# Six turns of the second block made by trips through memory and 32x32 block transpositions instead of TensorE transposes

## The chip, the cores and the metric

The kernel runs on one core of one Trainium2 chip. The metric is the time of one execution on the device in microseconds (us), median of several. PE is TensorE, DVE VectorE, ACT ScalarE, POOL GpSimd, SP SyncE; P is 128.

## The reference

The program computes a model of two blocks in fp32 on 256 tokens of width 1024. The first block has two layers of four mixers, a dense feed-forward part and a mixture of eight experts. The second block has two layers again, and each computes four branches of width 512 from one projection of the normalised input and joins them with one output projection:

```
y_ret = retention(rope(rq), rope(rk), rv) * silu(rg)
y_ssd = rmsnorm(ssd(silu(conv(xbc))) * silu(z)) * norm_g
y_stick = stick_breaking_attention(sq, sk, sv) * silu(sg)
y_mem = attention(mq, memory keys, memory values) * silu(mg)
h = h + rmsnorm(concat(y_ret, y_ssd, y_stick, y_mem) @ w_out)
```

`xbc` is 1024 wide: 512 state-space inputs x and two groups of B and C. Within ssd, the x part is used with tokens on the partitions; the convolution runs with features on the partitions.

## The kernel before

The five engines run hand-written instruction streams that meet at semaphores. Weights are fp32 and arrive by SP's DMAs in halves of 128x2048 in a ring of five. ACT rounds each half to its upper part (`split` on ACT, L2066) into one of four slots, DVE leaves the remainder in place (`split` on DVE, L2639), and PE adds three products of rounded operands for each weight: `weigh` (L1062) for tiles whose result has tokens on the partitions, `weigh_wide` (L1117, L1124) for results with features on the partitions. A half's upper part has to be there when PE starts on it, the remainder some 3.7 us later.

`SECOND_TILES` gives the order of the weight tiles in a layer of the second block, `SECOND_JOBS` (L324) the order in which results take the eight PSUM banks in turn: X0 X1 Z DT MQ MG SQ SK SV SG RQ RK RV RG, then the four tiles of the output projection, O1 O3 O2 O0. Between tiles PE does small work: maps (`causal`, L1663 and L1664), their application (`head_apply`, `ssd_apply`, L1669 to L1671), sums for the stick-breaking part (`stick_sums`, L1719, L1721), and turns.

A turn (`turn`, L1131) makes features-on-partitions of a 128x512 tile by four 128x128 transposes on PE into one bank; two such calls turn a 256x512 value. In each layer of the second block PE turns seven values, all by L1135: XT (x of the state-space part after the convolution, from features to tokens), the branches YM (memory), YD (state space), YS (stick-breaking) and YR (retention), and the rotated queries QR and keys KR of retention. Each ends in a bank, from which ACT copies it (XT, QR, KR) or takes its upper part (`y_high`, L2484) with DVE taking the remainder (`y_lower`, L3420).

DVE's stream in a layer is written out by hand in order. The part that matters here, between the splits of RK and O2: `stick_softplus`, `ssd_out(3)`, `y_lower` of YM, the normalisation of the state-space branch (L3603, L3604, then `ssd_n`), `rotate` of RQ (L3459 to L3463), `stick_out(0)`, `stick_softplus(2)`, split RV, `rotate` of RK, `stick_out(1)`, `stick_softplus(3)` (its last instruction, L3439, sets `sb_sp`, on which PE's `stick_sums(3)` waits), `y_lower` of YD, split RG, `stick_out(2)`, `stick_less(3)`, split O1, `stick_out(3)`, split O3, the decay of retention's maps LR0 to LR3 (L3634) with `y_lower` of YS between the second and the third.

POOL does almost nothing in the second block. In the dense feed-forward part of the first block it already carries six turns by another way, `store_rows` (L1950) and `fetch_pieces` (L1953): one DMA writes a 256x512 value to memory, then, when it has landed, four DMAs of 32 partitions each fetch it back so that each 32x32 piece lies in the partitions where its transpose belongs, and one DVE transposition of 32x32 blocks (L2972) finishes it:

```
pool.dma_start(dram.rearrange("(b p) d -> p b d", p=P), v).then_inc(moved_out, 16)
for a in range(QUADS):
    pool.dma_start(shaped(pieces, SEQ // GROUP, n)[GROUP * a:GROUP * (a + 1), :, :],
                   dram[:, n * a:n * (a + 1)].rearrange("(g j) c -> j g c", j=GROUP)).then_inc(fetched, 16)
```

POOL waits in its own order, so a trip starts only when the fetches of the one before have been issued.

Of the kernel before, what the change touches and what calls it, by code (L numbers as in the profile page):

```python
# [299 lines left out]
FFN_TURNS = 6  # L300

def expert_jobs(r):
# [113 lines left out]
def kernel_program(nc, t):  # L416
# [33 lines left out]
    with ctx:  # L450
# [275 lines left out]
        y_lows = [yr_low, yd_low, ys_low, ym_low]  # L726

        bank = [ctx.enter_context(nc.psum_tensor(f"bank{k}", [P, WIDE], F32)) for k in range(NBANK)]
        bias_dram = nc.dram_tensor("bias_by_distance", [MAPS, REL], F32, kind="Internal")
        hn_dram = nc.dram_tensor("normalised_rows", [SEQ, D], F32, kind="Internal")  # L730
        hid_dram = nc.dram_tensor("hidden_rows", [len(FF_PAIRS), SEQ, WIDE], F32, kind="Internal")
# [293 lines left out]
        def _(pe):  # L1025
# [627 lines left out]
            for l in range(LAYERS):  # L1653
# [126 lines left out]
                for b in range(TB):  # L1780
                    turn(f"XT{b}", [xbc[:, k, 3 + b * P:3 + (b + 1) * P] for k in range(4)], l)
# [27 lines left out]
                pe.wait_ge(*drained("XT1", l))  # L1809
# [22 lines left out]
                branch_turn("YM", gm, drained("PM3", l))  # L1832
# [9 lines left out]
                branch_turn("YD", zs, (ssd_n, l + 1))  # L1842
# [3 lines left out]
                for b in range(TB):  # L1846
                    pe.wait_ge(ret_q, at(l, 4, b + 1))
                    turn(f"QR{b}", [rq[:, b, k * P:(k + 1) * P] for k in range(4)], l)
                by_rows("RG", ["RG0", "RG1"])
                head_apply("PS3", sbw[:, 1, :], v2, 3, (sb_w, at(l, 4, 4)))  # L1850
                for b in range(TB):
                    pe.wait_ge(ret_q, at(l, 4, 2 + b + 1))
                    turn(f"KR{b}", [rk[:, b, k * P:(k + 1) * P] for k in range(4)], l)
# [7 lines left out]
                pe.wait_ge(*drained("YM1", l))  # L1861
# [6 lines left out]
                pe.wait_ge(*drained("YS1", l))  # L1868
# [22 lines left out]
        def _(pool):  # L1891
# [101 lines left out]
            for l in range(LAYERS):  # L1993
# [10 lines left out]
                pool.dma_start(ssd_row, t["ssd_norm_g_2"][l].partition_broadcast(P)).then_inc(rows_in, 16)  # L2004


        @block.scalar
        def _(act):
# [434 lines left out]
            for l in range(LAYERS):  # L2443
# [19 lines left out]
                def conv_silu(k):  # L2463
                    act.wait_ge(conv_acc, at(l, 8, 2 * k + 2))
                    for j in range(2):
                        c = 2 * k + j
                        ins = act.activation(xbc[:, c, 3:3 + SEQ], cacc2[:, k % 2, j, :], ACT.Silu,
                                             bias=par[:, 48 + c:49 + c])
                    ins.then_inc(conv_y, 1)
# [56 lines left out]
                copy2(xh[:, 0, :], "XT0")  # L2526
                copy2(xh[:, 1, :], "XT1")
# [3 lines left out]
                copy2(gm[:, 0, :], "MG0", func=ACT.Silu)  # L2531
                copy2(gm[:, 1, :], "MG1", func=ACT.Silu)
# [20 lines left out]
                copy2(g2[:, 0, :], "SG0", func=ACT.Silu)  # L2553
                copy2(g2[:, 1, :], "SG1", func=ACT.Silu)
# [4 lines left out]
                for b in range(TB):  # L2559
                    y_high(3, f"YM{b}", b)  # L2560
# [7 lines left out]
                inv_root(small2[:, 180:184], small2[:, 176:180], 256, ssd_sq)  # L2568
                stick_ln(2)
# [22 lines left out]
                for b in range(TB):  # L2592
                    y_high(2, f"YS{b}", b)
# [1128 lines left out]
```

## Time and profile before

| | |
|---|---|
| median of 3 runs | 2039.76 us (2037.66 to 2040.54) |
| the profiled execution | 2037.43 us, its span 2035.6 us |
| PE busy | 2023.8 us, 99% of the span, 17507 matmuls |
| DVE, ACT, POOL busy | 921.5 us (45%), 665.1 us (33%), 78.3 us (4%) |
| second block | from about 1540 us to the end, two layers of some 250 us |
| PE's granted clock | 0.999 of full |

Durations in the profile are of instructions one by one; PE's are pipelined and overlap, so that the time a group of matmuls takes is read from its start to the start of what follows.

### The profile page before, as it was taken

The numbers are of one execution on the slowest core, as the hardware profiler recorded it, in microseconds if no ns is written. First come the engines' busy times: TensorE is split into PE (matmuls) and PEld (weight loads), VectorE is DVE, ScalarE is ACT, GpSimd is POOL, SyncE is SP. The second block draws the span as 40 slices with busy tenths as digits, with TensorE's granted clock in tenths as the row PEclk, the third lists the DMA queues.
The fourth block names the chain that finished last, engine by engine and source line by source line (L and its number), as shares of the span: only waits on it lengthen the run. The fifth ranks groups of instructions, "written<-read, shape, count | busy, mean of one in ns | idle before, by whom it ended". The sixth has DMA issues, their size and how long they took to land.

```text
span 2035.6 us, 38980 instructions
## 1 busy us (share of the span) xinstructions
PE 2023.8 (99%) x17507; PEld 1348.0 (66%) x17507; DVE 921.5 (45%) x1286; ACT 665.1 (33%) x878; POOL 78.3 (4%) x113
## 2 busy tenths in 40 slices
PE   9999999999999999999999999999999999999998
PEld 6888888888888353434444353535357888888887
DVE  6877555577766110102020111110127777777775
ACT  5575544455655100000000000000005555456452
POOL 4100011000000000000000000000000000000000
PEclk9999999999999999999999999999999999999999
DMA  9654587555545999999999999999997544455342
GB/s 324 155 186 155 198 263 251 199 186 166 189 154 227 410 418 417 410 419 407 420 403 420 404 420 404 419 403 420 406 409 256 187 145 151 155 200 186 125 165 83
DMA packets 161934, 575.64 MB, mean 283 GB/s; under 512 B 13913, under 2 KB 26977, under 8 KB 130786
## 3 DMA queue, kind: packets, MB, share of 16 engines
q1 hardware_dynamic: 151040, 546.74, 71.3%
q0 software_dynamic: 7168, 22.01, 3.5%
q10 hardware_dynamic: 3554, 4.33, 0.6%
q8 instruction: 140, 2.29, 0.5%
q14 instruction: 32, 0.26, 0.0%
HBM read 564.76 MB, written 8.27 MB: 282 GB/s over the span
## 4 chain that ended last, share of the span: by engine, by line
PE 98%; DMA 1%; DVE 0%; ACT 0%; SPq 0%; DVEq 0%; issue 0%; ACTq 0%
PE bank L1062 40%; PE bank L1408 28%; PE bank L1440 13%; PE bank L1117 5%; PE bank L1124 3%; PE bank L1135 2%; PE bank L1068 1%; DMA ring<-moe_w_down 1%; PE bank L1161 0%; PE bank L1663 0%; PE bank L1671 0%; PE bank L1670 0%; PE bank L1691 0%; PE bank L1677 0%; PE bank L1669 0%; DMA ring<-w_in 0%
## 5 line engine op out<-in xcount | busy, mean ns | idle before, releaser
L1062 PE MATMUL bank<-halves_r,x_both 128*128 128x512 f32 x2624 | 606.8, 391 | 0.0
L1408 PE MATMUL bank<-ring,xT 128*32 128x512 f32 (+1 forms) x6144 | 580.4, 539 | 0.0
L1062 PEld LDWEIGHTS bank<-halves_r,x_both 128*128 128x128 f32 x2624 | 490.4, 188 | 102.0 <-issue 1.7
L1408 PEld LDWEIGHTS bank<-ring,xT 128*32 128x32 f32 x6144 | 199.1, 110 | 372.6 <-issue 371.2
L2639 DVE TENSOR_TENSOR halves_r<-ring,halves_r 128x2048 fp32r<-128x2048 f32 x170 | 384.2, 2287 | 129.0 <-ACT halves_r L2066 127.4
L2066 ACT ACTIVATE halves_r<-ring 128x2048 fp32r<-128x2048 f32 x172 | 325.5, 1914 | 189.7 <-DMA ring<-w_in 77.7
L3190 DVE TENSOR_TENSOR arena<-arena,bank 128x512 f32<-128x512 f32 (+1 forms) x48 | 29.7, 621 | 724.7 <-PE bank L1408 723.3
L1440 PE MATMUL bank<-ring,arena 128*32 128x256 f32 x5376 | 292.1, 379 | 0.7 <-DMA ring<-moe_w_down 0.6
L1440 PEld LDWEIGHTS bank<-ring,arena 128*32 128x32 f32 x5376 | 175.4, 110 | 117.3 <-issue 3.6
L2253 ACT ACTIVATE arena<-bank 128x512 f32<-128x512 f32 (+1 forms) x58 | 32.1, 553 | 462.1 <-PE bank L1408 429.9
L2331 ACT ACTIVATE arena<-bank 128x512 f32<-128x512 f32 (+1 forms) x14 | 6.1, 488 | 356.1 <-PE bank L1440 356.1
L1117 PE MATMUL bank<-x_both,halves_r 128*128 128x512 f32 x448 | 107.3, 392 | 0.3 <-DVE x_both L3486 0.3
L1117 PEld LDWEIGHTS bank<-x_both,halves_r 128*128 128x128 f32 x448 | 82.4, 188 | 18.4 <-issue 1.6
L1062 PE MATMUL bank<-halves_r,yT_high 128*128 128x512 f32 x256 | 80.7, 393 | 0.0
L1124 PEld LDWEIGHTS bank<-x_both,halves_r 128*128 128x128 f32 x448 | 57.4, 191 | 2.2
L1124 PE MATMUL bank<-x_both,halves_r 128*128 128x256 f32 x448 | 58.1, 283 | 0.0
L1062 PE MATMUL bank<-halves_r,hidT_high 128*128 128x512 f32 x176 | 54.7, 390 | 0.0
L1062 PEld LDWEIGHTS bank<-halves_r,yT_high 128*128 128x128 f32 x256 | 47.9, 188 | 9.8
L2044 ACT ACTIVATE arena<-bank 128x512 f32<-128x512 f32 x54 | 30.8, 597 | 61.5 <-PE bank L1062 50.0
L1981 POOL DMA_INDIRECT arena<-normalised_rows,arena x21 | 20.0, 951 | 795.2 <-DVEq L3211 791.0
L3194 DVE STREAM_TRANSPOSE arena<-arena 128x512 f32<-128x512 f32 (+1 forms) x48 | 45.8, 1004 | 0.0
L2645 DVE TENSOR_REDUCE arena<-bank 128x256 f32<-128x512 f32 x56 | 35.1, 683 | 13.9 <-PE bank L1124 13.8
(423 smaller groups left out, 1577.9 us busy)
## 6 DMA issues: line engine op xcount, KB each, us to landing
ring<-moe_w_gate_up SPq DMA_DIRECT2D x128, 1024.0 KB, 13.1
ring<-moe_w_down SPq DMA_DIRECT2D x112, 1024.0 KB, 12.3
ring<-w_in SPq DMA_DIRECT2D x99, 1024.0 KB, 5.2
ring<-moe_w_gate_up SPq DMA_DIRECT2D x128, 768.0 KB, 9.1
ring<-w_out SPq DMA_DIRECT2D x24, 1024.0 KB, 4.9
ring<-ffn_w_gate_up SPq DMA_DIRECT2D x20, 1024.0 KB, 5.5
ring<-ffn_w_down SPq DMA_DIRECT2D x11, 1024.0 KB, 5.0
ring<-w_in SPq DMA_DIRECT2D x18, 512.0 KB, 6.1
```

What stands on the lines that cost most here:

```text
L1062: return pe.matmul(o[:, a:a + n], x[:, c, b * P:(b + 1) * P], w[:, k, col:col + n], **flags)
L1117: mm = pe.matmul(shaped(o[:, :], 2, SEQ), w[:, k, j * P:(j + 1) * P], x_pair[:, :, c, :], start=c == 0, stop=False)
L1124: mm = pe.matmul(o[:, 0:SEQ], w[:, k, j * P:(j + 1) * P], xT_high[:, c, :], start=False, stop=c == KC - 1)
L1135: mm = pe.transpose(o[:, k * P:(k + 1) * P], v, order)
L1408: mm = pe.matmul(shaped(o[i][GROUP * z:GROUP * (z + 1), 0:u], u // P, P), xg[:, c, GROUP * i:GROUP * (i + 1)], w[:, q, z, :, :], start=c == 0,
L1440: mm = pe.matmul(o[i // 2][GROUP * q:GROUP * (q + 1), Q_D * (i % 2):Q_D * (i % 2 + 1)], hidT_m[half][:, i, b:b + GROUP], w[:, c, Q_D * q:Q ...
L2044: act.activation(dst, src, func, scale=scale).then_inc(*fr(job))
L2066: act.activation(top_view(half), raw_view(half), ACT.Copy).then_inc(top_in, 1)
L2253: act.activation(dst, out_of(job)[:, 0:n], ACT.Silu).then_inc(*fr(job))
L2639: dve.tensor_tensor(raw_view(half, halves_r), raw_view(half), top_view(half).bitcast(F32), ALU.subtract).then_inc(raw_low_in, 1)
L2645: dve.tensor_reduce(dst, out_of(job)[:, :].rearrange("p (t s) -> p s t", s=SEQ), AX.X, ALU.add).then_inc(*fr(job))
L3194: dve.transpose(hidT_m[half][:, i, :].rearrange("p (t c g) -> p t c g", c=4, g=GROUP), gated[half][:, i, :].rearrange("p (t f c) -> p t c ...
```

## The change

Six of the seven turns of each layer (all but YR) leave PE. PE's transposes, their twelve places in the order of banks and the copies out of the banks go. In their place each value makes the trip on POOL's queue in the order XT, YM, YD, QR, KR, YS, with a store of 512 KB and four fetches of 128 KB; DVE transposes it in one instruction (XT in two), and for the branches ACT and DVE then take upper part and remainder from SBUF, one 128x1024 instruction each. To let the fetches take whole runs, the producers write their value with the columns in another order (`by_quarter`), in runs of 32 elements: ACT's activations for the convolution, MG and SG, DVE's `mem_out`, `stick_out`, `rotate` and the last factor of the state-space norm, which is now two instructions that write to `xh`.

```diff
+SECOND_TURNS = ('XT', 'YM', 'YD', 'QR', 'KR', 'YS')
+def turns_up_to(l, name):
+    return FFN_TURNS + l * len(SECOND_TURNS) + SECOND_TURNS.index(name) + 1
...
     # PE
-                for b in range(TB):
-                    turn(f"XT{b}", [xbc[:, k, 3 + b * P:3 + (b + 1) * P] for k in range(4)], l)
...
-                pe.wait_ge(*drained("XT1", l))
+                pe.wait_ge(pieces_turned, turns_up_to(l, "XT"))
...
-                branch_turn("YM", gm, drained("PM3", l))
...
-                branch_turn("YD", zs, (ssd_n, l + 1))
...
-                for b in range(TB):
-                    pe.wait_ge(ret_q, at(l, 4, b + 1))
-                    turn(f"QR{b}", [rq[:, b, k * P:(k + 1) * P] for k in range(4)], l)
...
-                pe.wait_ge(*drained("YD1", l))
+                pe.wait_ge(rest_in, FFN_TURNS + at(l, 3, 2))
                 out_tile(1, first=True)
-                pe.wait_ge(*drained("KR1", l))
-                pe.wait_ge(*drained("QR1", l))
+                pe.wait_ge(pieces_turned, turns_up_to(l, "KR"))
...
-                branch_turn("YS", g2, drained("PS3", l))
...
     # POOL
+                sources = {"XT": (xh, flat(xbc[:, 0:4, :])[:, 0:TB * WIDE], (conv_y, at(l, 4, 2))),
+                           "QR": (rq, rq, (ret_q, at(l, 4, 2))), "KR": (rk, rk, (ret_q, at(l, 4, 4))),
+                           "YM": (gm, gm, drained("PM3", l)), "YD": (xh, zs, (ssd_n, l + 1)), "YS": (g2, g2, drained("PS3", l))}
+                for name in SECOND_TURNS:
+                    source, pieces, ready = sources[name]
+                    dram = turn_dram.ap()[l, SECOND_TURNS.index(name)]
+                    pool.wait_ge(*ready)
...
+                    store_rows(dram, source)
+                    pool.wait_ge(moved_out, 48 + 16 * turns_up_to(l, name))
+                    fetch_pieces(dram, flat(pieces))
...
     # ACT
+                def y_top(n):
+                    k = turned_order[n]
+                    act.wait_ge(pieces_turned, turns_up_to(l, ("YM", "YD", "YS")[n]))
+                    act.activation(yT_high[:, 4 * k:4 * k + 4, :], branch_whole[n], ACT.Copy).then_inc(y_in, 1)
...
-                for b in range(TB):
-                    y_high(1, f"YD{b}", b)
                 split(("RG", l))
+                y_top(1)
...
     # DVE
+                def y_turn(n):
+                    dve.wait_ge(fetched, 16 + 16 * QUADS * turns_up_to(l, ("YM", "YD", "YS")[n]))
+                    dve.transpose(branch_whole[n].rearrange("p k (g j) -> p g k j", j=GROUP),
+                                  pieces_of(flat(branch_pieces[n]))).then_inc(pieces_turned, 1)
+                def y_rest(n):
+                    k = turned_order[n]
+                    dve.wait_ge(y_in, at(l, 5, n + 1))
+                    dve.tensor_tensor(y_lows[k][:, :, :], branch_whole[n],
+                                      yT_high[:, 4 * k:4 * k + 4, :].bitcast(F32), ALU.subtract).then_inc(rest_in, 1)
...
-                link(dve.tensor_tensor(zs[:, :, :], zs[:, :, :], under(ssd_row, TB), ALU.mult))
+                for b in range(TB):
+                    ins = dve.tensor_tensor(by_quarter(xh[:, b, :]), in_order(zs[:, b, :]), in_order(ssd_row), ALU.mult)
+                link(ins)
...
                 rotate("RQ1", rq, 1)
+                y_rest(0)
...
-                for b in range(TB):
-                    y_lower(1, f"YD{b}", b, 2 + b)
+                y_turn(1)
                 split(("RG", l))
+                y_rest(1)
                 stick_out(2)
                 stick_less(3)
+                head_rows_turn("QR", q2T, rq)
                 split(("O1", l))
                 stick_out(3)
+                head_rows_turn("KR", k2T, rk)
                 split(("O3", l))
                 for hd in range(4):
                     if hd == 2:
-                        for b in range(TB):
-                            y_lower(2, f"YS{b}", b, 4 + b)
+                        y_turn(2)
+                        y_rest(2)
                         split(("O2", l))
```

On PE, between the tiles RK and RV of a layer (names are tiles; `arena` holds most values), before:

```order
L1719 MATMUL bank<-soft_r,ge_r 128x384
L1721 MATMUL bank<-soft_r,sums_r 128x256 x2
L1135 MATMUL bank<-consts,arena 128x128 [waits bank_free5,ssd_n]
L1135 MATMUL bank<-consts,arena 128x128 x3
L1135 MATMUL bank<-consts,arena 128x128 [waits bank_free6,ssd_n]
L1135 MATMUL bank<-consts,arena 128x128 x3
L1062 MATMUL bank<-halves_r,x_both 128x512 [waits top_in,bank_free0,bank_free7]
```

and in the change:

```order
L1730 MATMUL bank<-soft_r,ge_r 128x384
L1732 MATMUL bank<-soft_r,sums_r 128x256 x2
L1062 MATMUL bank<-halves_r,x_both 128x512 [waits top_in,bank_free2,bank_free1]
```

The eight transposes of YD and their wait on `ssd_n` are gone, and the next tile takes other banks.

On DVE, from the end of `stick_softplus(3)` through the splits of RG and O1, before:

```order
L3439 TENSOR_TENSOR soft_r<-arena,soft_r 128x384 [waits dve_step]
L3420 TENSOR_TENSOR yd_low<-bank,yT_high 128x4x128 [waits y_in] x2
L2639 TENSOR_TENSOR halves_r<-ring,halves_r 128x2048 [waits top_in] x2
L3453 TENSOR_TENSOR arena<-bank,arena 128x2x128 [waits bank_full1,bank_free5]
L3445 TENSOR_TENSOR arena<-arena,bank 128x384 [waits bank_full2]
L2639 TENSOR_TENSOR halves_r<-ring,halves_r 128x2048 [waits dve_step,top_in]
```

and in the change:

```order
L3467 TENSOR_TENSOR soft_r<-arena,soft_r 128x384 [waits dve_step]
L3436 STREAM_TRANSPOSE arena<-arena 128x8x4x32 [waits fetched]
L2656 TENSOR_TENSOR halves_r<-ring,halves_r 128x2048 [waits top_in] x2
L3442 TENSOR_TENSOR yd_low<-arena,yT_high 128x1024 [waits y_in]
L3481 TENSOR_TENSOR arena<-bank,arena 128x8x32 [waits bank_full3,bank_free3]
L3473 TENSOR_TENSOR arena<-arena,bank 128x384 [waits bank_full4]
L3498 STREAM_TRANSPOSE arena<-arena 128x8x4x32 [waits dve_step,fetched]
L2656 TENSOR_TENSOR halves_r<-ring,halves_r 128x2048 [waits top_in] x2
```

The transposition of YD stands where its subtractions from the bank stood; the subtraction now comes after the split of RG, and the transposition of QR is new.

On POOL, the last three trips of a layer in the change, where nothing stood before:

```order
L1950 DMA turned_rows<-arena 128x2x512 [waits ret_q]
L1955 DMA arena<-turned_rows 32x8x128 [waits moved_out]
L1955 DMA arena<-turned_rows 32x8x128 x3
L1950 DMA turned_rows<-arena 128x2x512 [waits ret_q]
L1955 DMA arena<-turned_rows 32x8x128 [waits moved_out]
L1955 DMA arena<-turned_rows 32x8x128 x3
L1950 DMA turned_rows<-arena 128x2x512 [waits bank_free7]
L1955 DMA arena<-turned_rows 32x8x128 [waits moved_out]
L1955 DMA arena<-turned_rows 32x8x128 x3
```

They are QR, KR and YS; each first fetch waits for its own store, and each store stands behind the fetches of the trip before.

## Rows read from the trace of the kernel before

**Rows 1.** Busy time, share and instructions of each engine, the page's first part.

```profile
PE 2023.8 (99%) x17507; PEld 1348.0 (66%) x17507; DVE 921.5 (45%) x1286; ACT 665.1 (33%) x878; POOL 78.3 (4%) x113
```

**Rows 2.** The chain that ended last, by engine.

```profile
PE 98%; DMA 1%; DVE 0%; ACT 0%; SPq 0%; DVEq 0%; issue 0%; ACTq 0%
```

**Rows 3.** Waits of PE in the second block: waited for, us, times, longest.

```profile
PE bank L1135 <- DVE xs L2624: 0.6, 1, 0.6
PE bank L1117 <- DVE x_both L3486: 0.3, 1, 0.3
```

**Rows 4.** Timeline of PE, layer 0: start, us, engine, line, tiles; XT, then YM.

```profile
1600.91 1.07 PE L1135 MATMUL bank<-consts,arena 128*128 128x128 f32 x8
1601.82 0.60 PE L1663 MATMUL bank<-arena 128*128 128x256 f32 x2
...
1676.15 1.04 PE L1135 MATMUL bank<-consts,arena 128*128 128x128 f32 x8
1676.95 11.18 PE L1062 MATMUL bank<-halves_r,x_both 128*128 128x512 f32 x48
```

**Rows 5.** The same in layer 1: XT.

```profile
1850.74 1.07 PE L1135 MATMUL bank<-consts,arena 128*128 128x128 f32 x8
1851.65 0.60 PE L1663 MATMUL bank<-arena 128*128 128x256 f32 x2
```

**Rows 6.** Timeline of DVE in layer 0.

```profile
1616.23 0.69 DVE L3356 TENSOR_REDUCE arena<-bank 128x2 f32<-128x512 f32 x1 [4.83 <-PE bank L1677]
...
1676.34 4.49 DVE L2639 TENSOR_TENSOR halves_r<-ring,halves_r 128x2048 fp32r<-128x2048 f32 x2 [0.24 <-ACT halves_r L2066]
...
1683.64 1.28 DVE L3420 TENSOR_TENSOR ym_low<-bank,yT_high 128x512 fp32r<-128x512 f32 x2
...
1687.85 1.23 DVE L3604 TENSOR_TENSOR arena<-arena 128x1024 f32<-128x1024 f32 x1
...
1692.52 0.41 DVE L3460 TENSOR_TENSOR xs<-bank,arena 128x256 f32<-128x256 f32 x1
...
1693.41 0.69 DVE L3463 TENSOR_TENSOR arena<-xs 128x512 f32<-128x512 f32 x1
...
1711.88 0.56 DVE L3439 TENSOR_TENSOR soft_r<-arena,soft_r 128x384 fp32r<-128x384 f32 x1
...
1728.48 0.42 DVE L3453 TENSOR_TENSOR arena<-bank,arena 128x256 f32<-128x256 f32 x1 [4.38 <-PE bank L1671]
...
1740.87 1.21 DVE L3634 TENSOR_TENSOR arena<-bank,arena 128x384 f32<-128x384 f32 x2 [6.20 <-PE bank L1664]
```

**Rows 7.** One DVE transposition of the feed-forward part, min/median/max ns.

```profile
L2972 DVE STREAM_TRANSPOSE arena<-arena x6: 706/1236/1239, 280.2 to 371.8; 128x1024 f32<-128x1024 f32 x5, 128x512 f32<-128x512 f32 x1
```

**Rows 8.** Timeline of ACT: a copy of 128x1024.

```profile
1540.56 1.06 ACT L2489 ACTIVATE arena<-xT 128x1024 f32<-128x1024 f32 x1
```

**Rows 9.** Timeline of PE in layer 0: the last stick-breaking sums, the map LR2.

```profile
1715.09 0.59 PE L1719 MATMUL bank<-soft_r,ge_r 128*128 128x384 f32 x2
...
1753.13 0.59 PE L1663 MATMUL bank<-arena 128*128 128x256 f32 x2
```

**Rows 10.** Timeline of POOL: two of the six trips of the feed-forward part.

```profile
260.82 0.73 POOL L1951 DMA_DIRECT2D hidden_rows<-arena  x1 [42.17 <-DVE arena L2990]
265.79 2.37 POOL L1956 DMA_DIRECT2D arena<-hidden_rows  x4 [4.23 <-DMA hidden_rows<-arena]
280.84 0.72 POOL L1951 DMA_DIRECT2D hidden_rows<-arena  x1 [12.69 <-DVE arena L2990]
288.02 2.33 POOL L1956 DMA_DIRECT2D arena<-hidden_rows  x4 [6.45 <-DMA hidden_rows<-arena]
```

**Rows 11.** Everything on the tile `hidden_rows`: issues in ns, and landings.

```profile
L1956 POOL DMA_DIRECT2D arena<-hidden_rows x24: 582/582/646, 265.8 to 363.3; - x24
...
DMA to landing us min/median/max: 3.0/4.4/6.9
```

**Rows 12.** Busy time by stretch: the feed-forward trips, and layer 0 here.

```profile
250.00:370.00 120.00, 120.00 (x531) 99.41 (x530) 70.75 (x45) 54.90 (x40) 18.36 (x30) 1.00 0.80 256
1560.00:1780.00 220.00, 220.00 (x1192) 189.20 (x1191) 169.76 (x267) 114.11 (x158) 0.53 (x1) 1.00 0.51 165
```

More of the change, by code:

```diff
@@ L726, in kernel_program @@
         y_lows = [yr_low, yd_low, ys_low, ym_low]
+        turned_order = (3, 1, 2)
+        branch_pieces = [gm, zs, g2]
+        branch_whole = [shaped(flat(v), 4, SEQ) for v in (xs[:, 1:2, :], xh, v2)]
         bank = [ctx.enter_context(nc.psum_tensor(f"bank{k}", [P, WIDE], F32)) for k in range(NBANK)]
@@ L730, in kernel_program @@
         hn_dram = nc.dram_tensor("normalised_rows", [SEQ, D], F32, kind="Internal")
+        turn_dram = nc.dram_tensor("turned_rows", [LAYERS, len(SECOND_TURNS), SEQ, WIDE], F32, kind="Internal")
         hid_dram = nc.dram_tensor("hidden_rows", [len(FF_PAIRS), SEQ, WIDE], F32, kind="Internal")
@@ L2466, in conv_silu @@
                         c = 2 * k + j
-                        ins = act.activation(xbc[:, c, 3:3 + SEQ], cacc2[:, k % 2, j, :], ACT.Silu,
-                                             bias=par[:, 48 + c:49 + c])
+                        if c < 4:
+                            dst = flat(xh).rearrange("p (a c b q) -> p c b a q", a=QUADS, c=4, b=TB)[:, c]
+                            src = shaped(cacc2[:, k % 2, j, :], TB, QUADS, GROUP)
+                        else:
+                            dst, src = xbc[:, c, 3:3 + SEQ], cacc2[:, k % 2, j, :]
+                        ins = act.activation(dst, src, ACT.Silu, bias=par[:, 48 + c:49 + c])
                     ins.then_inc(conv_y, 1)
@@ L2552, in _ @@
                 seg_exponential(3)
-                copy2(g2[:, 0, :], "SG0", func=ACT.Silu)
-                copy2(g2[:, 1, :], "SG1", func=ACT.Silu)
+                copy2(by_quarter(g2[:, 0, :]), "SG0", func=ACT.Silu)
+                copy2(by_quarter(g2[:, 1, :]), "SG1", func=ACT.Silu)
                 split(("RK", l))
@@ L2580, in _ @@
                 stick_exp(3)
-                for b in range(TB):
-                    copy2(q2T[:, :, b * P:(b + 1) * P], f"QR{b}")
                 for b in range(TB):
@@ L2589, in _ @@
                 log_exp()
-                for b in range(TB):
-                    copy2(k2T[:, :, b * P:(b + 1) * P], f"KR{b}")
-                for b in range(TB):
-                    y_high(2, f"YS{b}", b)
+                y_top(2)
                 split(("O2", l))
@@ L3462, in rotate, with head_rows_turn @@
                     dve.sem_inc(*fr(job))
-                    link(dve.tensor_tensor(shaped(dst[:, b, :], 4, P), ra, rb, ALU.add))
+                    link(dve.tensor_tensor(by_quarter(dst[:, b, :]), in_order(rope_t[:, 0, :]), in_order(rope_t[:, 1, :]),
+                                           ALU.add))
                     dve.sem_inc(ret_q, 1)
+                def head_rows_turn(name, dst, src):
+                    dve.wait_ge(fetched, 16 + 16 * QUADS * turns_up_to(l, name))
+                    dve.transpose(dst.rearrange("p k (g j) -> p g k j", j=GROUP),
+                                  pieces_of(flat(src))).then_inc(pieces_turned, 1)
                 if l == 1:
@@ L3550, in _ @@
                 split(("SQ", l))
+                dve.wait_ge(fetched, 16 + 16 * QUADS * turns_up_to(l, "XT"))
+                x_pieces2 = flat(xbc[:, 0:4, :])[:, 0:TB * WIDE].rearrange("p (g c b q) -> p b c g q", g=QUADS, c=4, b=TB)
+                for b in range(TB):
+                    ins = dve.transpose(xh[:, b, :].rearrange("p (c g j) -> p c g j", c=4, g=QUADS), x_pieces2[:, b])
+                ins.then_inc(pieces_turned, 1)
                 dve.wait_ge(*full("AC", l))
@@ L3596, in _ @@
                 ssd_out(3)
-                for b in range(TB):
-                    y_lower(3, f"YM{b}", b, b)
+                y_turn(0)
                 dve.wait_ge(ssd_sq, l + 1)
@@ L3603, in _ @@
                     link(dve.tensor_tensor(z, z, over(s2[:, 180 + 2 * b:182 + 2 * b], 256), ALU.mult))
-                link(dve.tensor_tensor(zs[:, :, :], zs[:, :, :], under(ssd_row, TB), ALU.mult))
+                for b in range(TB):
+                    ins = dve.tensor_tensor(by_quarter(xh[:, b, :]), in_order(zs[:, b, :]), in_order(ssd_row), ALU.mult)
+                link(ins)
                 dve.sem_inc(ssd_n, 1)
```

37 lines of the change are left out of this document (20 added, 17 removed), and 6 rows, old and new, of the table SECOND_JOBS.

## The prediction

> **What bounds the kernel.** I read the page first: PE is busy for 2023.8 of 2035.6 us, DVE for 45% and ACT for a third [rows 1]. The chain that ended last says the same more strictly, since it follows releases: 98% of it is PE [rows 2]. So an instruction that leaves PE is worth its time unless PE then has to wait. The view of waits, cut to the second block, tells how near PE is to waiting: it waits twice in some 500 us, for 0.6 and 0.3 us, both ahead of the first turn that the change touches [rows 3]. Last I read the timelines of PE and DVE through one layer. The stretch view shows DVE at 169.8 of 220 us there, 77%, and the DMA engines at 0.51 [rows 12]: DVE, 45% over the whole span, is the engine to watch in this block.
>
> **What is removed from PE.** Each turn is eight transposes. Their own durations overlap, so I take start to start. XT starts at 1600.91 and the next work at 1601.82, 0.91 us; YM at 1676.15 and the next tile at 1676.95, 0.80 us [rows 4]. YD, QR, KR and YS have the same shape and take 0.79 each. A layer thus loses 0.91 + 0.80 + 4 x 0.79 = 4.87 us, and layer 1 shows the same 0.91 for XT [rows 5]. Two layers: 9.74 us, 96 matmuls. The small gaps when PE changes from one kind of work to another stay, because the small work around the turns stays.
>
> **What is added to DVE.** The nearest row for a transposition is the very same operation on the very same shape in the feed-forward part, 1.24 us for 128x1024 [rows 7]. Per layer:
> - YM, YD, YS: the transposition (1.24) takes the place of the two subtractions (1.28, rows 6), and one subtraction of 128x1024 comes later. Its nearest row is L3604, 1.23 us for the same size [rows 6]. Net +1.2 each.
> - QR, KR: +1.24 each. XT: two of 128x512, about 1.4.
> - The norm's last factor, 1.23 us in one instruction, becomes two of 128x512 at 0.69 (L3463), +0.15 [rows 6].
> Together some 7.7 us per layer on an engine with about 50 us idle in it. ACT gets lighter: three pairs of copies from banks go, and each branch has one copy of 1.06 us [rows 8] instead of two. Writing in runs of 32 I take at nothing: L3460 writes 256 elements in four runs of 64 in 0.41 us, at the rate of the contiguous 128x512 in 0.69 [rows 6]. The bounds are 0 and a doubling of every such instruction; the row is much nearer to 0.
>
> **Where DVE's additions lie.** XT's 1.4 us falls before 1616.23, where DVE had been idle for 4.83 us waiting for PE [rows 6]; it costs nothing. The tight place is from 1676 to 1712. It starts with the split of RK at 1676.34, which follows ACT, which follows PE's end of the tile SG; PE is by then earlier by XT's 0.91, and DVE with it. From there DVE has hardly a gap to the end of `stick_softplus(3)`, 1711.88 + 0.56 = 1712.44. The change adds 0.15 and 1.23 less about 0.2 that fills a gap between dependent instructions: 1712.44 - 0.91 + 1.18 = 1712.7, with a release around 1712.8. PE wants this for the sums that began at 1715.09 [rows 9], less XT, YM and YD, 2.50: at 1712.6. So a slack of 2.65 us is spent, and I expect 0.2 us of waiting, in both layers: 0.4 us. What follows on PE, the tile RG, needs its upper half from ACT, whose stream gets there by the same chain but does RG's split before YD's copy now; I add nothing. Behind it DVE has 4.38 us idle before 1728.48 [rows 6], which covers the later subtraction (1.2) and QR's transposition (1.2).
>
> **The trips.** From the store's issue to the first fetch's issue 4.97 and 7.18 us [rows 10]; the last of four fetches is issued 1.75 us later (2.33 less one issue of 0.58, rows 10, 11); it lands 3.0 to 6.9 us after that, 4.4 in the middle [rows 11]. A trip t is so 9.7 to 15.8 us, 12.2 in the middle. The DMA engines were at 0.80 there and are at 0.51 here [rows 12]; the change adds 12 x 0.5 MB per layer, about 27 GB/s on 165, so I lean to the lower half. Weight loads share the DMA engines, but ACT splits most halves several us before PE wants them; I take nothing for it.
> - YD may start when the norm ends, 1689.1, and DVE wants it at 1712.4: 23 us.
> - QR and KR queue behind it on POOL. A trip holds POOL for t - 3.8, so KR lands at about 1689.2 + 3t - 7.6, 1718 at t = 12.2; DVE wants it after 1728.9 - 3.3 = 1725.6.
> - YS is the tightest. It starts when `stick_out(3)` ends (1728.90 before), and DVE wants it after LR1, 1740.87 + 1.21 = 1742.08, of which KR's 0.79 goes: 12.4 us. A later landing makes DVE wait, with the split of O2 and the maps LR2 and LR3 behind it. After landing DVE needs 1.24, ACT's 1.06, 1.23 and O2's 4.49, 8.0 us. LR2 is on PE at 1753.13 + 0.8 before, 1752.4 without KR and YS, which is 23.5 after `stick_out(3)`. So t up to 15.5 costs PE nothing.
>
> **Sum.** 9.74 - 0.4 = 9.3 us. The profiled execution, 2037.43 with a span of 2035.6, becomes 2028.1; it lies 2.3 under the median of 2039.76. On the median: **2030.5**. Its own range, with 0 to 2 us of waiting per layer and the scatter of the runs (2037.66 to 2040.54), is 2028.5 to 2033. What a measurement can tell from no change is about 0.2%, 4.1 us.
>
> **Rivals.**
> 1. DVE becomes the bound in the tight place. If runs of 32 double the instructions that write them, the two of the norm, four of `rotate` and two of `stick_out` add 2 x 0.69 + 4 x 0.69 + 2 x 0.42 = 5.0 us per layer; no slack is left, so all of it reaches PE, 10.0 us in two layers: 2040.5. Half of it: 2035.5. For it: the slack is spent already. Against it: L3460's rate. Chance 0.11, 0.05 of it beyond 2035.7.
> 2. YS lands late, t of 16 to 17. PE waits 1 to 3 us per layer: 2034.5. For it: 15.8 is the feed-forward part's worst. Against it: less traffic here. 0.07.
> 3. Slower. The trips run one behind the other, so lateness adds up: YD, QR, KR, YS in a row land YS at 1689.2 + 4t - 11.4, and PE can do without it until about 1742.4. Beyond t = 16.2 each us of t costs 4 us per layer. The gain of 4.65 per layer is gone at t = 17.4; t = 19 gives 2030.5 + 2 x 11.2 = 2053. For it: nothing of this traffic has been on POOL in this block, beside a DVE at 77%. Against it: 24 issues in the feed-forward part lie at 582 to 646 ns [rows 11], with DVE at 71 of 120 us [rows 12], so neither issue nor landing shows a busy DVE. 0.04.
> The Trainium skill, page "SBUF — State Buffer", section "SBUF: two separate sides", has a rule that speaks for this rival: while DVE runs one of its two-port modes, GpSimd can't write the descriptors of its own DMAs, and they wait. By that rule the trips would be longer than in rows of an idle DVE; the steady 582 ns next to a DVE at 59% does not bear it out.
> 4. The change does less than it says, because PE's transposes ran in time that PE would have waited anyway. With no wait in rows 3 behind them this would show as no change, 2039.8. 0.01.
>
> **How the numbers follow.** Forecast 0.77, rival 1 0.11, rival 2 0.07, rival 3 0.04, rival 4 0.01. Faster by over 0.2%: 0.77, 0.06 of rival 1 and 0.05 of rival 2, together 0.88; slower by over 0.2%: 0.04; within 0.2%: the remaining 0.08. The range from 2028 to 2035.5 holds the forecast, rival 2 and the mild half of rival 1.
>
> **What would show it.** PE has 17411 matmuls and is still at 98 to 99%. No L1135 between the tiles but for YR and the turns of maps. PE waits under 1 us at `stick_sums(3)` and nowhere else. Stores and fetches of `turned_rows` within 16 us per trip. DVE gains some 15 us of busy time, with transpositions of 1.24 us. I am wrong if PE waits several us for `pieces_turned` or `rest_in` (rivals 2, 3), if DVE's instructions in runs of 32 are longer than their twins (rival 1), or if weight halves reach ACT late.

## The result, and the profile after

| | before | changed |
|---|---|---|
| median of 6 runs each | 2037.68 us (2036.49 to 2040.54) | 2027.57 us (2026.15 to 2029.02) |
| ratio, 95% interval | | 0.995 (0.994 to 0.996) |
| profiled execution: time, span | 2037.43, 2035.6 us | 2029.02, 2027.2 us |
| second block, from PE's first work on the step sizes (4 matmuls of 128x8) in its first layer to the end | 2035.6 - 1600.55 = 435.05 us | 2027.2 - 1601.88 = 425.32 us |
| from layer to layer on PE (the same 4 matmuls in the second layer, less those in the first) | 1850.38 - 1600.55 = 249.83 us | 1846.88 - 1601.88 = 245.00 us |

The change makes the kernel 10.1 us faster by the medians, 9.7 us by the trace of the second block. I forecast 9.3. The median lies all the same 0.43 us below the range of 2028.0 to 2035.5, for a reason that has little to do with the change (below). The two last lines of the table are the better measure: what lies ahead of this point wanders by more than a microsecond from run to run (it was reached at 1600.55 before and, in runs of the changed kernel, at 1599.34 to 1601.88), and none of the work that leaves PE is there. Of the kernel before there is one trace, so 435.05 and 249.83 stand on one execution.

The page of the changed kernel, its first part and the chain by engine, which answer to [rows 1, 2]:

```profile
PE 2015.9 (99%) x17411; PEld 1337.9 (66%) x17411; DVE 934.5 (46%) x1296; ACT 658.1 (32%) x860; POOL 114.2 (6%) x173
...
PE 97%; DMA 2%; DVE 1%; ACT 0%; issue 0%; DVEq 0%; POOL 0%; SPq 0%; ACTq 0%; POOLq 0%
```

PE has 96 instructions fewer and is still the chain. DVE has 13 us more (I had said some 15) and POOL 36; what of it reaches PE is looked at below. The waits of PE in the second block are the two of [rows 3], no more:

```profile
PE bank L1146 <- DVE xs L2641: 0.6, 1, 0.6
PE bank L1128 <- DVE x_both L3521: 0.3, 1, 0.3
```

The stretch of [rows 12] in layer 0. The DMA share goes from 0.51 to 0.62 and the traffic from 165 to 202 GB/s, 37 more where I had said some 27; where the other 10 come from was not looked into:

```profile
1560.00:1780.00 220.00, 220.00 (x1184) 188.87 (x1183) 179.93 (x279) 115.40 (x155) 18.55 (x31) 1.00 0.62 202
```

PE around `stick_sums(3)` (L1730, L1732 now), in the timeline: the product before it begins at 1713.74, the sums 0.38 us later, where 0.14 is usual between the same two kinds of work (1701.56 to 1701.70). So PE starts 0.24 us late there, which the view of waits doesn't show, and it is the one new wait. (The ends of matmuls are modelled in the profile, so I go by starts.)

```profile
1701.56 0.38 PE L1675 MATMUL bank<-arena 128*128 128x128 f32 x2
1701.70 0.60 PE L1730 MATMUL bank<-soft_r,ge_r 128*128 128x384 f32 x2
...
1713.74 0.39 PE L1682 MATMUL bank<-arena 128*128 128x128 f32 x2
1714.12 0.62 PE L1730 MATMUL bank<-soft_r,ge_r 128*128 128x384 f32 x2
```

DVE in layer 0. L3467 is the end of the fourth softplus, which PE waits for, L3436 and L3442 the transposition and the subtraction of a branch, L3498 the transposition of QR, L3492 and L3481 the last addition of `rotate` and the product of `stick_out`, which write in runs of 32 now and take the 0.69 and 0.42 us that they took before [rows 6]:

```profile
1706.85 0.69 DVE L3492 TENSOR_TENSOR arena<-xs 128x512 f32<-128x512 f32 x1
...
1709.89 0.42 DVE L3481 TENSOR_TENSOR arena<-bank,arena 128x256 f32<-128x256 f32 x1
...
1713.51 0.56 DVE L3467 TENSOR_TENSOR soft_r<-arena,soft_r 128x384 fp32r<-128x384 f32 x1
1713.98 1.24 DVE L3436 STREAM_TRANSPOSE arena<-arena 128x1024 f32<-128x1024 f32 x1
...
1721.77 1.25 DVE L3498 STREAM_TRANSPOSE arena<-arena 128x1024 f32<-128x1024 f32 x1 [0.24 <-DMA arena<-turned_rows]
...
1739.63 1.25 DVE L3436 STREAM_TRANSPOSE arena<-arena 128x1024 f32<-128x1024 f32 x1 [0.15 <-DMA arena<-turned_rows]
1742.01 1.23 DVE L3442 TENSOR_TENSOR ys_low<-arena,yT_high 128x1024 fp32r<-128x1024 f32 x1 [1.13 <-ACT yT_high L2506]
1743.81 4.49 DVE L2656 TENSOR_TENSOR halves_r<-ring,halves_r 128x2048 fp32r<-128x2048 f32 x2 [0.58 <-ACT halves_r L2083]
1750.51 1.21 DVE L3678 TENSOR_TENSOR arena<-bank,arena 128x384 f32<-128x384 f32 x2 [2.21 <-PE bank L1675]
```

The transposition at 1739.63 is YS. DVE waits for its landing, but only 0.15 us, and 2.21 us of idle time are left before LR2. POOL's store of YS, and the fetch issues of all second-block trips but XT's, in ns (min/median/max):

```profile
1728.02 0.72 POOL L1950 DMA_DIRECT2D turned_rows<-arena  x1 [10.46 <-DVE arena L3481]
```

```profile
L1955 POOL DMA_DIRECT2D arena<-turned_rows x40: 582/582/613, 1666.2 to 1979.2; - x40
```

Stored at 1728.02, transposed at 1739.63: this trip takes 11.6 us at most, where I took 12.2 for the middle. The fetch issues take 582 ns in the median, as in [rows 11], with DVE busy for 82% of the stretch, so this DVE work doesn't make them longer. The rule that I had weighed for rival 3 (the Trainium skill, page "SBUF — State Buffer", section "SBUF: two separate sides") is one on DVE's two-port modes. No row tells how much of DVE's work here ran in one, so the runs neither bear out nor refute the rule itself.

### The profile page after: what moved, and what is told of

The parts are those of the page before. It is cut to its first block, busy times and chain, and to the rows that moved or that the text cites. A ratio compares the mean times of both kernels' runs of the same rounds, so it can differ in the third digit from the quotient of the medians.

```text
span 2027.2 us, 38820 instructions
## 1 busy us (share of the span) xinstructions
PE 2015.9 (99%) x17411; PEld 1337.9 (66%) x17411; DVE 934.5 (46%) x1296; ACT 658.1 (32%) x860; POOL 114.2 (6%) x173
## 4 chain that ended last, share of the span: by engine, by line
PE 97%; DMA 2%; DVE 1%; ACT 0%; issue 0%; DVEq 0%; POOL 0%; SPq 0%; ACTq 0%; POOLq 0%
PE bank L1073 40%; PE bank L1419 29%; PE bank L1451 13%; PE bank L1128 5%; PE bank L1135 2%; PE bank L1146 1%; PE bank L1079 1%; DMA ring<-moe_w_down 1%; DMA ring<-w_in 1%; PE bank L1674 0%; PE bank L1172 0%; PE bank L1681 0%; PE bank L1682 0%; PE bank L1702 0%; PE bank L1688 0%; PE bank L1680 0%
## 5 line engine op out<-in xcount | busy, mean ns | idle before, releaser
L2061 ACT ACTIVATE arena<-bank 128x512 f32<-128x512 f32 x42 | 24.2, 594 | 57.0 <-PE bank L1073 46.3
```

The costliest lines, as they stand in the source:

```text
L2061: act.activation(dst, src, func, scale=scale).then_inc(*fr(job))
```

## The experiments

Eleven runs were made, two of them of the changed kernel itself, in three groups (e1 to e4, e5 to e8, e9 to e11), each group on one chip with the kernel before beside it. The medians of before were 2036.74 us (15 runs) for the first group, 2037.27 (15) for the second and 2037.52 (9) for the third. For each I give the median and, from its trace, the two distances of the table above: from layer to layer on PE, and from the first of these points to the end ("second block"). For the kernel before they are 249.83 and 435.05.

| kernel | median | under before | layer to layer | second block |
|---|---|---|---|---|
| e1_again | 2026.67 | 10.1 | 245.05 | 425.46 |
| e2_rest_later | 2027.37 | 9.4 | 244.64 | 424.65 |
| e3_dve_extra | 2033.33 | 3.4 | 247.94 | 430.79 |
| e4_store_twice | 2044.50 | -7.8 | 256.82 | 445.02 |
| e5_no_trips | 2029.09 | 8.2 | 245.05 | 425.44 |
| e6_ys_twice | 2038.58 | -1.3 | 250.30 | 435.51 |
| e7_ys_on_pe | 2029.65 | 7.6 | 245.92 | 427.26 |
| e8_mem_trips | 2024.90 | 12.4 | 242.94 | 421.18 |
| e9_ys_twice_o2_first | 2026.93 | 10.6 | 245.07 | 425.50 |
| e10_best | 2023.88 | 13.6 | 242.97 | 421.24 |
| e11_again | 2028.24 | 9.3 | 245.03 | 425.35 |

The last two columns repeat within 0.15 us for kernels that do the same work on PE (e1, e5, e9, e11; 0.2 us with the first trace of the changed kernel), while the medians of these four spread over 2.4 us. Small effects are read from the trace.

### The changed kernel again

> The changed kernel, unchanged. My theory: the change gives 9.3 us, as forecast, and the 10.1 us by which the first measured median lay below that of before came partly from the three runs of before that the forecast was set on (2037.66 to 2040.54). So against before, in runs taken side by side, 8.8 to 10.2 us, ratio 0.995 to 0.996. Rival: the sum is mis-sized and the gain is 11 us or more, which would show as a ratio of 0.9946 or less, and as more than 9.8 us in the trace between the start of the second block on PE and the end.

Measured: 10.1 us under before, ratio 0.9953 (0.994 to 0.9967). The same kernel in the third group, e11_again, gave 9.3 us, 0.9957 (0.9943 to 0.997).

> The changed kernel once more, on the same chip and beside the same runs of before as e10_best, so that the two can be set side by side: 9.3 to 10.1 us under before, and 3.5 to 4.5 us over e10_best; from the start of the second block to the end 425.3 to 425.5 us in the trace.

Both lie in or at the edge of what was expected, and no trace of it shows more than 9.8 us. The gain is 9.3 to 10.1 us, and the rival of a gain of 11 us falls. But my theory that the first 10.1 came partly from the runs of before isn't borne out: 15 other runs of before gave 10.1 again.

### Is the tight stretch without slack?

```
                 rotate("RQ1", rq, 1)
-                y_rest(0)
                 stick_out(0)
...
                 split(("RG", l))
+                y_rest(0)
                 y_rest(1)
```

> YM's subtraction (1.22 us) is taken out of DVE's tight stretch and done just ahead of YD's, where DVE is idle. Theory (the stretch from RK's split to the fourth softplus has no slack left, PE waits 0.24 us for it): the gap on PE ahead of stick_sums(3), 0.38 us from start to start now, falls to its usual 0.14; 0.2 to 0.3 us less per layer, 0.5 us in all, 2027.1 where the unchanged kernel shows 2027.6. Rival (the 0.24 us come from something else, such as the matmul queue or the weight load): the gap stays at 0.38, no change in time. Only the trace can tell the two apart, since 0.5 us is less than the scatter of the runs.

PE's timeline of this kernel: the sums follow after 0.14 us. The layer is 0.41 us shorter than in e1_again.

```profile
1712.72 0.39 PE L1682 MATMUL bank<-arena 128*128 128x128 f32 x2
1712.86 0.59 PE L1730 MATMUL bank<-soft_r,ge_r 128*128 128x384 f32 x2
```

The wait is therefore DVE's, and it costs 0.4 us per layer rather than 0.24, more than I had expected: the products right behind the sums move closer too. The medians (2027.37 against 2026.67) don't show it. The opposite edit adds work to the same stretch:

```
+                    for again in range(3 if job in ("RQ0", "RQ1") else 1):
                         link(dve.tensor_tensor(by_quarter(dst[:, b, :]), ..., ALU.add))
```

> Four more instructions of 0.69 us on DVE per layer (the last addition of the rotation of RQ0 and RQ1 is done three times instead of once), 2.8 to 3.0 us per layer in the tight stretch. Theory (no slack is left between DVE's stretch and the fourth stick_sums on PE): PE waits 2.7 to 3.2 us longer per layer ahead of stick_sums(3), or partly at the stick_sums before it; 5 to 6.5 us slower than the unchanged kernel, 2033 to 2034. Rival (there is slack, or gaps between DVE's dependent instructions swallow the addition): 0 to 2 us slower.

Four instructions of 0.69 us more per layer, 2.8 in all, make the first layer 2.89 us longer and the two together 5.3 (430.79 against 425.46); by the medians the kernel is 6.7 us slower than e1_again. Nearly every added microsecond reaches PE. But the place is another than I had written. PE waits in the second block:

```profile
PE bank L1680 <- ACT arena L2501: 3.9, 4, 1.3
PE bank L1730 <- DVE soft_r L3467: 0.5, 2, 0.2
```

PE now waits mainly for the exponentials (L2501) ahead of PS1 and PS2, which ACT can compute only after `stick_less` on DVE. So the stretch feeds PE at several points. How much room each had stands in the timelines of e1_again, the exponential on ACT and the product (L1680) that wants it:

```profile
1695.94 0.51 ACT L2501 ACTIVATE arena<-arena 128x384 f32<-128x384 f32 x1
1697.95 0.38 PE L1680 MATMUL bank<-arena 128*128 128x128 f32 x2
...
1709.88 0.51 ACT L2501 ACTIVATE arena<-arena 128x384 f32<-128x384 f32 x1
1710.78 0.38 PE L1680 MATMUL bank<-arena 128*128 128x128 f32 x2
```

1.5 us ahead of PS1 and 0.4 ahead of PS2, and none at the sums behind PS2. A delay of 2.8 us uses up the first two as well: PE waits 1.29 and 0.81 us there in layer 0.

### Do the trips cost anything?

```
-                for name in SECOND_TURNS:
+                for name in ("XT",):
...
-                    dve.wait_ge(fetched, 16 + 16 * QUADS * turns_up_to(l, name))
+                    dve.wait_ge(*readies[name])
```

> Left out: the stores and fetches of YM, YD, QR, KR and YS; DVE transposes what lies in the buffers as soon as the rows are ready, so that the branches and the retention compute on rows that are not turned. PE, DVE and ACT do the same instructions as in the changed kernel. Theory (with trips of 9 to 12 us the trips cost PE nothing, and their traffic disturbs nobody): within 0.5 us of the changed kernel, and the distance from layer to layer on PE stays at 245.0 us, since the 0.38 us that remain at stick_sums(3) come from DVE's own work. Rival (the traffic of 40 to 50 GB/s delays weight tiles, or landings delay DVE somewhere on the path): 1 to 3 us faster.

This kernel leaves out the stores and fetches of all values but XT, so DVE transposes rows as they lie and the results are not those of the model; the instructions on PE, ACT and DVE are the same. Without ten of the twelve trips the layer takes 245.05 us, as with them, and the second block 425.44 against 425.46. These trips and their traffic are free. (The median, 2029.09, is higher than e1_again's. With traces this equal I read nothing from it.)

### How far are they from costing something?

```
...
                     store_rows(dram, source)
-                    pool.wait_ge(moved_out, 48 + 16 * turns_up_to(l, name))
+                    pool.wait_ge(moved_out, 32 * turns_up_to(l, name) - 64)
+                    store_rows(dram, source)
+                    pool.wait_ge(moved_out, 32 * turns_up_to(l, name) - 48)
```

> Every one of the six turns of each layer stores its rows twice, the second store after the first has landed, so that each trip is longer by some 2.5 to 4 us and GpSimd's queue with it. The values stay the same. Theory (trips are serial; now about 9 to 12 us each, and the last one, YS, has about 4 us to spare before PE waits for its product; XT has more): trips of 12 to 15 us, four of them in a row from YD on, land YS at 1741 to 1750 on the time scale of the changed kernel's trace, and PE waits 0 to 4 us per layer ahead of the first causal product of the retention or ahead of tile O2: 0 to 8 us slower in all, 2 likeliest. Rival of free trips (they never reach PE): within 0.3 us of the unchanged kernel and no new wait of PE in the trace. Rival of tight trips (PE waits at LR0 for KR): more than 8 us slower.

This is far off: 7.8 us slower than before and 17.8 slower than the changed kernel, with its five runs from 2039.7 to 2048.1. My likeliest case was 2, and the rival of more than 8 had PE wait at LR0 for KR, which it doesn't. POOL, DVE and PE in layer 0, and the waits:

```profile
1729.07 0.72 POOL L1950 DMA_DIRECT2D turned_rows<-arena  x1
1737.10 0.72 POOL L1950 DMA_DIRECT2D turned_rows<-arena  x1 [7.31 <-DMA turned_rows<-arena]
1743.67 2.34 POOL L1955 DMA_DIRECT2D arena<-turned_rows  x4 [5.86 <-DMA turned_rows<-arena]
```

```profile
1748.86 1.25 DVE L3440 STREAM_TRANSPOSE arena<-arena 128x1024 f32<-128x1024 f32 x1 [10.02 <-DMA arena<-turned_rows]
...
1757.44 1.01 DVE L3682 TENSOR_TENSOR arena<-bank,arena 128x384 f32<-128x384 f32 x2
```

```profile
PE bank L1680 <- DVE arena L3682: 14.0, 2, 8.9
```

```profile
1758.14 0.77 PE L1680 MATMUL bank<-arena 128*128 128x128 f32 x2 [8.93 <-DVE arena L3682]
...
1763.40 0.55 PE L1073 MATMUL bank<-halves_r,yT_high 128*128 128x512 f32 x1
```

PE waits 8.93 us in layer 0 and 5.1 in layer 1 for LR2's product, which stands on DVE behind YS and the split of O2. KR was late as well (DVE idle for 7.27 us before it), without reaching PE. The second block is 19.6 us longer than in e1_again. 14.0 of these are waits; where are the other 5.5? The stretches, with the granted clock third from the end:

```profile
1749.00:1758.00 9.00, 0.21 (x2) 0.01 (x1) 7.30 (x6) 7.86 (x5) 0.00 (x0) 0.75 0.24 92
1758.00:1763.40 5.40, 5.26 (x19) 4.71 (x20) 3.41 (x19) 0.81 (x3) 0.00 (x0) 0.50 0.00 0
1763.40:1770.00 6.60, 6.60 (x30) 5.46 (x29) 6.57 (x11) 0.00 (x0) 0.00 (x0) 0.97 0.07 24
```

Behind the wait the clock is at 0.50, its lower level of 1.2 GHz, for 5.4 us of work in layer 0: half of it, 2.7 us, is lost on top of the wait, and about as much in layer 1, which makes up the 5.5. To separate YS from the row of trips before it:

```
...
                     store_rows(dram, source)
...
+                    if name == "YS":
+                        store_rows(dram, source)
+                        pool.wait_ge(moved_out, 64 + 16 * l + 16 * turns_up_to(l, name))
```

> Only YS, the last trip of a layer, stores its rows twice, one store after the other; the values stay the same. The trip gets 4 to 5.5 us longer (11.6 us now). From the changed kernel's trace: DVE takes YS within 0.2 us of its landing, and what is behind it has 2.2 us of idle time before LR2 and 1.1 us more until PE wants the product of LR2, 3.3 us together. Theory: PE waits 0.7 to 2.2 us per layer ahead of the third PR, nowhere else, and its clock stays up since the wait is short: 1.5 to 4.5 us slower than the changed kernel, 3 likeliest. Rival (the clock falls with this wait too, as it did behind the waits of 5.1 and 8.9 us, where 2.8 us per layer were lost on top): 6 to 10 us slower. Rival (it was the row of late trips before YS, not YS itself, that cost the time when all stores were doubled): within 0.5 us.

The doubled store of YS alone, one of six in each layer, costs 10.05 us in the second block: the whole gain. POOL's store, DVE's transposition of YS, PE's waits, and the stretches behind the wait in layer 0:

```profile
1725.88 0.72 POOL L1950 DMA_DIRECT2D turned_rows<-arena  x1 [10.39 <-DVE arena L3484]
```

```profile
1744.46 1.25 DVE L3439 STREAM_TRANSPOSE arena<-arena 128x1024 f32<-128x1024 f32 x1 [7.11 <-DMA arena<-turned_rows]
```

```profile
PE bank L1680 <- DVE arena L3681: 6.4, 2, 3.4
```

```profile
1753.70:1755.00 1.30, 1.25 (x11) 1.28 (x12) 1.26 (x5) 0.30 (x1) 0.00 (x0) 1.00 0.00 0
1755.00:1758.60 3.60, 3.60 (x12) 2.83 (x12) 2.84 (x17) 0.42 (x2) 0.00 (x0) 0.53 0.00 0
```

The trip takes 18.6 us, 7.0 more than the 11.6, where I expected 4 to 5.5 more. The second store took 6.9 us to its release, the first 4.5. A busy DVE is not the reason: it was busy for all of the 4.5 us, but for only 1.75 of the 6.9. What is, no run tells. Against 3.3 us of slack that gives a wait of 3.7; measured are 3.41 and 3.02. The rival on the clock holds: it falls after waits of this size too, though only 1.3 us after PE has resumed at 1753.75, and takes 10.05 - 6.43 = 3.6 us from the two layers. The rival that only the row before YS was to blame falls.

### Order instead of speed

```
                     if hd == 2:
+                        split(("O2", l))
                         y_turn(2)
                         y_rest(2)
-                        split(("O2", l))
```

and the same on ACT with `y_top(2)`, both on top of e6_ys_twice.

> YS stores its rows twice as in e6_ys_twice (which cost 10 us in the trace), but ACT and DVE split the tile O2 before they take YS, not after. Theory: the cost of a late YS came from the order of the two engines, not from the lateness: O2's split (3.7 us on ACT, 4.5 on DVE) then fills the time in which DVE waited 7 us for the landing, and only the transposition, ACT's copy and the subtraction, 3.6 us, stand between the landing and LR2's multiplication. With YS on DVE at about 1744.5 and PE wanting LR2's product at 1750.2 PE waits for nothing: the distance from layer to layer returns to 245.0 to 245.3 us, within 1 us of the changed kernel. Rival (O2's tile is not in the ring that early, or ACT is late with it, so that YS now waits behind O2): PE waits again, 2 us or more per layer.

DVE's timeline:

```profile
1739.39 4.48 DVE L2659 TENSOR_TENSOR halves_r<-ring,halves_r 128x2048 fp32r<-128x2048 f32 x2
1746.50 1.25 DVE L3439 STREAM_TRANSPOSE arena<-arena 128x1024 f32<-128x1024 f32 x1 [2.62 <-DMA arena<-turned_rows]
...
1750.51 1.21 DVE L3681 TENSOR_TENSOR arena<-bank,arena 128x384 f32<-128x384 f32 x2 [0.41 <-PE bank L1675]
```

The same slow trip of 18.5 us (1728.01 to 1746.50) costs nothing: 245.07 us per layer, and the kernel is 10.6 us under before, where e6_ys_twice was 1.3 over it. What cost the time was not the late landing by itself but the split of O2 queued behind it. The changed kernel has YS 3.3 us from costing something; in this order 7 us more are harmless.

### What a turn on PE is worth

> YS is turned by PE again, as before the change (8 transposes, two copies by ACT, two subtractions by DVE from the banks); the other five stay with the trips. Theory of the sum (each turn is worth its own time on PE, 0.79 us): the distance from layer to layer on PE rises from 245.0 to 245.8 us, the kernel is 1.6 us slower than the changed one. Rival (YS's trip costs PE something in the changed kernel, so that its removal gave less than 0.79): 0 to 1 us slower.

YS is back on PE, with its old copies and subtractions. The layer is 0.87 us longer, not 0.79, and the second block 1.8 us (427.26 against 425.46) where I expected 1.6. PE's timeline of this kernel, and then of the changed one at the same place:

```profile
1737.28 0.38 PE L1675 MATMUL bank<-arena 128*128 128x128 f32 x2
1737.50 1.04 PE L1146 MATMUL bank<-consts,arena 128*128 128x128 f32 x8
1738.30 0.48 PE L1073 MATMUL bank<-halves_r,yT_high 128*128 128x512 f32 x1
```

```profile
1738.50 0.38 PE L1675 MATMUL bank<-arena 128*128 128x128 f32 x2
1738.64 0.48 PE L1073 MATMUL bank<-halves_r,yT_high 128*128 128x512 f32 x1
```

With the turn 1.02 us pass from the last causal product to the tile, without it 0.14: 0.88. The turn's own start to start is 0.80; the other 0.08 us lie ahead of it, since the transposes begin 0.22 us after the product and the tile only 0.14.

That holds where a turn stood between such a product or sum and a tile. XT stood elsewhere, between the work on the step sizes and the first map. PE there before, around the turn [rows 4], and in the changed kernel:

```profile
1600.55 0.51 PE L1575 MATMUL bank<-arena 128*128 128x8 f32 x4
...
1602.26 0.38 PE L1664 MATMUL bank<-arena 128*128 128x128 f32 x2
```

```profile
1601.88 0.51 PE L1586 MATMUL bank<-arena 128*128 128x8 f32 x4
...
1602.76 0.38 PE L1675 MATMUL bank<-arena 128*128 128x128 f32 x2
```

1.71 us before, 0.88 after: XT's turn was worth 0.83, not the 0.91 from its start to the map's, because the map's own first part, 0.44 us to the next start before [rows 4], now takes 0.52.

### A better version

The memory attention's maps still had 16 transposes per layer on PE. e8_mem_trips turns them by two more trips, each with one DVE transposition of 128x1024, and has YM's subtraction later:

```
-SECOND_TURNS = ('XT', 'YM', 'YD', 'QR', 'KR', 'YS')
+SECOND_TURNS = ('XT', 'AMa', 'AMb', 'YM', 'YD', 'QR', 'KR', 'YS')
...
                 segment_maps(1)
+                head_rows_turn("AMa", pmT, probs[0])
...
                 split(("SG", l))
+                head_rows_turn("AMb", pmT, probs[1])
                 segment_maps(2)
```

> A candidate for a better kernel: YM's subtraction moved as in e2_rest_later, and the four maps of the memory attention (16 transposes on PE per layer, 0.87 us for each pair by the changed kernel's timeline) are turned by two further trips, one per pair, with one DVE transposition of 128x1024 each; ACT loses four copies. DVE has idle time of 4 us and more where the two transpositions go, and the trips have 17 and 20 us. Theory: 1.74 + 0.4 = 2.1 us less per layer on PE, the distance from layer to layer falls from 245.0 to 242.9 us, the kernel is 4.2 us faster than the changed one, 2022 to 2023. Rival (the writes in runs of 32 by ACT, or DVE's added work, push a split back, and PE waits): 0 to 2 us faster, with a wait of PE ahead of the third or fourth PM.

242.94 us per layer, as expected, and 421.18 us for the block, 4.3 less than e1_again. The median is 2024.9 us, 2 over the 2022 to 2023 expected, 12.4 under before, ratio 0.9936 (0.9923 to 0.995). PE's waits are still the same two. DVE finds the first of the two trips landed and takes it without a wait; behind it 0.88 us of idle time are left:

```profile
1639.41 1.24 DVE L3493 STREAM_TRANSPOSE xs<-xs 128x1024 f32<-128x1024 f32 x1
1641.52 2.48 DVE L2657 TENSOR_REDUCE arena<-bank 128x256 f32<-128x512 f32 x4 [0.88 <-PE bank L1136]
```

> e8_mem_trips with O2 split ahead of YS as well. Theory: on fast trips the order of YS and O2 changes nothing for PE, the distance from layer to layer stays at 242.9 us, and the time is that of e8_mem_trips: 4.2 us under the changed kernel in the trace of the second block, 3.5 to 4.5 in the medians. Rival (YS is now taken later and pushes something back): up to 2 us slower than e8_mem_trips.

With O2 ahead of YS as well: 2023.88 us, 4.4 us under the changed kernel beside it (e11_again), 13.6 under before, ratio 0.9932 (0.9919 to 0.9946). In the trace it equals e8_mem_trips (421.24 and 421.18), and the lower median lies within the scatter of the runs. That O2's earlier split makes it less sensitive to a slow trip is shown for the changed kernel (e9_ys_twice_o2_first), not for this one.

## Why the prediction was right, and where it failed

- **What bounds the kernel, and that a turn is worth its time on PE**: right. PE's instructions fell by 96 and the chain is still PE. Rival 4 is out.
- **The six turns, 4.87 us per layer**: too small by 0.3. Without the wait (e2_rest_later) a layer is 249.83 - 244.64 = 5.19 us shorter. I took the time from the first transpose to the next work, 0.79, and wrote that the small gaps around stay; e7_ys_on_pe shows 0.08 us ahead of a turn that goes with it. Laid side by side, the timelines of before and of e2_rest_later give 0.88 us for each of YD, QR, KR and YS, but 0.83 for YM and for XT, where I had 0.80 and 0.91.
- **0.2 us of waiting at `stick_sums(3)` in both layers**: right place, right cause (e2_rest_later), 0.24 us at the wait itself and 0.4 in its effect. e3_dve_extra shows how close the reckoning of "no slack" was, but also that it isn't one point: the exponentials ahead of PS1 and PS2 had only 1.5 and 0.4 us.
- **Sum**: 2 x (5.19 - 0.38) is 9.6 us, the trace 9.7, the forecast 9.3. That it comes so near is partly luck: the turns were 0.6 too small and the wait 0.3 to 0.4 too small, and half of the one cancels against the other.
- **Runs of 32 at nothing** (rival 1): right, 0.69 and 0.42 us as before.
- **The trips** (t of 12.2, YS free up to 15.5): right. YS took 11.6 us in the changed kernel. Delayed on purpose, it gave waits of 3.41 and 3.02 us at t = 18.6 and 18.2, where t - 15.5 is 3.1 and 2.7. For the row of trips rival 3 said that each microsecond beyond 16.2 costs 4; in e4_store_twice YD is stored at 1686.70 and YS transposed at 1748.86, which by its 4t - 11.4 is t = 18.4, so 8.8 us of waiting against 8.93 measured. In layer 1 the same kernel waited 5.1 us. The mechanisms of rivals 2 and 3 exist as described, in kernels made to show them. Their prices were too low: neither had the clock, which took 1.8 to 2.8 us per layer on top.
- **From the sum to the median: here it failed.** "It lies 2.3 under the median of 2039.76. On the median: **2030.5**." That median was of three runs. With three more it was 2037.68, and in 39 further runs of before in three groups 2036.74 to 2037.52; the anchor was 2 to 3 us too high. Of the 2.9 us between 2030.5 and the measured 2027.57 the anchor makes 2.1 and the gain (10.1 by the medians, not 9.3) 0.8. The profiled execution of 2037.43 was near the middle. Its own forecast, 2028.1, is 0.5 us from the measured 2027.57. The range failed with it: its low end, 2028.0, lies only 0.4 under the fastest of the three runs less the forecast gain (2037.66 - 9.3 = 2028.4), so it had room neither for an anchor too high nor for a gain too small.

## What to carry to other kernels

On a bound engine, price a piece by the start of the work before it and the start of the work after it, with and without the piece, not by its own duration; and look one start further, since the work behind it can get longer. For a new wait, ask what is queued behind the waiting instruction before asking how late the landing is: one swap of order made 7 us of lateness free. And a forecast in absolute time is no better than the median it stands on; with three runs some microseconds apart, the range owes that spread on both sides.

## What the runs showed of the hardware

The granted clock falls from 1.00 to 0.50 with a standstill of PE of 3.0 to 8.9 us (e4_store_twice, e6_ys_twice). In the waits of 8.9 and 5.1 us it fell while PE stood still: in layer 0 it is 1.00 from 1749.0 to 1753.4 and 0.50 from 1753.6 to 1758.0. In the waits of 3.0 and 3.4 us it fell 0.8 and 1.3 us after PE had resumed. It was back at 1.00 4.1 to 5.6 us after PE had resumed, with 3.4 to 5.6 us of work at 0.50 behind each wait. Waits of 0.8 to 1.3 us (e3_dve_extra) cost little beyond themselves: the clock stays at 1.00, and only the first product behind them takes 0.1 us more. So in this kernel a wait of 3 us costs about 5, which neither the prediction nor the expectation of e4_store_twice had.

The landing of the same 512 KB store varies a lot. In the changed kernel 3.4 to 8.5 us pass from a store's issue to the first fetch; in e6_ys_twice two stores of the same rows back to back took 4.5 and 6.9 us. The slow landing was beside the idler DVE. What else sets it was not tried.
